# Three rounded passes for the query, key and value up-projections, and three weight splits moved ahead of their blocks

## What is computed

```python
# first layer: latent attention, sparse attention, gates, output projection
c_q = rmsnorm(c_q, mla_q_norm_g)                       # 512 x 384
q_a = einsum('bsr,re->bse', c_q, w_uq)                 # 8 heads x 96
c_kv = rmsnorm(c_kv, mla_kv_norm_g)                    # 512 x 256
k_nope = einsum('bsr,re->bse', c_kv, w_uk)             # 8 heads x 64
v_a = einsum('bsr,re->bse', c_kv, w_uv)                # 8 heads x 64
...
y = sigmoid(g_a) * (o_a @ w_o_a) + sigmoid(g_b) * (o_b @ w_o_b)
x = x + y @ w_out                                      # 1024 x 1024
...
# second layer: feed-forward with a 3-tap convolution
u = causal_dwconv(h @ ffn_up, ffn_dw)                  # 1024 -> 2 x 2816
y = (silu(u[..., 2816:]) * u[..., :2816]) @ ffn_down   # 2816 -> 1024
```

## Time and profile before

| | |
|---|---|
| median of 3 runs | 2231.27 us (2227.53 to 2238.28) |
| the profiled execution | 2231.33 us, span 2229.6 us |
| mean granted TensorE clock | 0.93 of full |
| PE busy | 1988.4 us, 89% of the span, 14734 matmuls |
| PE weight load (PEld) | 1689.8 us, 76% |
| DVE (VectorE) | 1311.2 us, 59% |
| ACT (ScalarE) | 945.0 us, 42% |
| POOL (GpSimd) | 711.1 us, 32% |
| HBM | 239.10 MB read, 116 GB/s over the span |

### The profile page before, as it was taken

How to read it: one execution, slowest core, us unless ns; L and a number is a source line. 1 busy time by engine, 2 the same in 40 slices (tenths; PEclk the granted TensorE clock), 3 DMA queues, 4 the chain that set the end, 5 groups by cost and what they waited for, 6 DMA issues and landing times. The chain is left out here.

```text
span 2229.6 us, 36859 instructions
## 1 busy us (share of the span) xinstructions
PE 1988.4 (89%) x14734; PEld 1689.8 (76%) x14734; DVE 1311.2 (59%) x1946; ACT 945.0 (42%) x1485; POOL 711.1 (32%) x378
## 2 busy tenths in 40 slices
PE   6999998799799997598999796688899989999797
PEld 4777644575677776598999575688689979999684
DVE  3779645432789897505999475565421167887402
ACT  4234258523788887522222543233333153232322
POOL 2433300131121111143433164421135425555441
PEclk9999988899899999699999897799789999999899
DMA  4222210022999998223223013210132212222231
GB/s 175 86 78 92 67 48 1 29 85 77 369 350 370 353 364 301 86 87 121 88 86 134 29 48 99 45 31 13 40 115 93 78 57 95 88 93 86 70 100 38
DMA packets 89378, 260.09 MB, mean 117 GB/s; under 512 B 26304, under 2 KB 27472, under 8 KB 88464
## 3 DMA queue, kind: packets, MB, share of 16 engines
q1 hardware_dynamic: 85488, 247.90, 32.1%
q0 software_dynamic: 3744, 10.11, 1.3%
HBM read 239.10 MB, written 18.87 MB: 116 GB/s over the span
## 5 line engine op out<-in xcount | busy, mean ns | idle before, releaser
L1546 DVE TENSOR_TENSOR moe_wlo<-moe_ring,moe_whi 128x1024 fp32r<-128x1024 f32 x198 | 234.0, 1219 | 43.4 <-ACT moe_whi L1542 40.5
L528 PE MATMUL acc<-h_xhi,h_whi 128*128 128x264 f32 x816 | 234.5, 287 | 13.1 <-DVE h_xlo L463 7.2
L528 PE MATMUL acc<-h_xlo,h_whi 128*128 128x264 f32 x816 | 233.5, 286 | 0.0
L528 PE MATMUL acc<-h_xhi,h_wlo 128*128 128x264 f32 x816 | 233.3, 286 | 0.0
L1542 ACT ACTIVATE moe_whi<-moe_ring 128x1024 fp32r<-128x1024 f32 x198 | 203.6, 1058 | 37.2 <-PE acc L1602 19.2
L528 PE MATMUL acc<-ff_xhi,ff_whi 128*128 128x258 f32 x704 | 200.8, 285 | 9.4 <-DVE ff_xlo L463 9.4
L528 PE MATMUL acc<-ff_xhi,ff_wlo 128*128 128x258 f32 x704 | 199.8, 284 | 0.0
L528 PE MATMUL acc<-ff_xlo,ff_whi 128*128 128x258 f32 x704 | 199.7, 284 | 0.0
L395 POOL TENSOR_TENSOR h_wlo<-ring,h_whi 128x1024 fp32r<-128x1024 f32 x49 | 117.5, 2400 | 201.7 <-ACT h_whi L387 201.7
L528 PEld LDWEIGHTS acc<-h_xhi,h_whi 128*128 128x128 f32 x816 | 156.1, 191 | 14.4 <-DVE h_xlo L463 8.3
L1986 DVE SCALAR_TENSOR_TENSOR acc<-cp,par,acc 128x528 f32<-128x528 f32 x232 | 159.2, 765 | 0.0
(11 more groups left out here) (506 smaller groups left out, 5158.4 us busy)
## 6 DMA issues: line engine op xcount, KB each, us to landing
ring<-slabs SPq DMA_DIRECT2D x213, 512.0 KB, 3.4
moe_ring<-moe_slabs SPq DMA_DIRECT2D x204, 512.0 KB, 5.7
tok_rows<-h_tok SPq DMA_DIRECT2D x5, 512.0 KB, 4.3
h_spill<-x2r SPq DMA_DIRECT2D x1, 2112.0 KB, 6.6
v_spill<-rw_v SPq DMA_DIRECT2D x1, 2112.0 KB, 7.4
y_spill<-cp SPq DMA_DIRECT2D x8, 264.0 KB, 4.6
rw_v<-v_spill SPq DMA_DIRECT2D x1, 2112.0 KB, 8.1
x2r<-h_spill SPq DMA_DIRECT2D x1, 2112.0 KB, 8.4
```

The costliest lines, as they stand in the source:

```text
L528: mm = nc.tensor.matmul(acc[j][0:rows, s, 0:t1 - t0], wp[:, at:at + rows], xp[:, t0:t1], start=(k == 0 and m == 0), stop=(k == kt - 1 and ...
L1546: tensor_tensor(wlo[u % AHEAD][:, :], ringm[u % RAW][:, :], whi[u % AHEAD][:, :].bitcast(F32), ALU.subtract).then_inc(w_lo[u % 2], 1)
```

## The change

1. The weights' buffers of the input block are made before `normalize("mix")`, and the first two c_q slabs are split there: ScalarE rounds the first after its eight squares and the second after the root; GpSimd subtracts both.
2. The up-projections take three rounded passes. The latents get an `Operand` each (`cq` 3 tiles, `ckv` 2). Slabs 1 and 2 of w_uq are split at the end of the gates' block, the other four (w_uq's third, two of w_uk, one of w_uv) inside the block, between read-outs on ScalarE and between the key copies on GpSimd.
3. w_out joins the block of w_o_a and w_o_b: `yo_xhi` and `yo_xlo` are made tile by tile as sums become ready, and TensorE goes on from w_o_b to w_out without a barrier.
4. ffn_down joins the block of ffn_up: 8 of the 22 `hid` tiles are split during ffn_up, 14 after its last tile; ffn_down's first two slabs are split before ffn_up's last tiles are read out.

Core of the diff (line numbers of the kernels differ by some lines after the first hunk):

```diff
-            if name not in ("w_uq", "w_uk", "w_uv", "wa_up", "g_up"):
+            if name not in ("wa_up", "g_up"):
...
+                        if split and enter:
+                            split[0].act(act, split[0].ahead(split[1])[0])
                         wait(act, sq_used, kt)
                         nc.scalar.activation(fold(std[:, :], t), A(1, t), ACT.Sqrt,
                                              bias=k0("eps", 1, eps)).then_inc(rooted, 1)
+                        if split and enter:
+                            split[0].act(act, split[0].ahead(split[1])[1])
...
                         tile_loop(act, w, [(name, KD, 8) for name in g_names], take)
+                        for n in w.ahead("w_uq"):
+                            w.act(act, n)
...
-                    pe_tiles(pe, None, "w_uq", 3, HEADS, lambda k: cc[:, k, :], T1, up_ready, up_out, rows=96)
-                    pe_tiles(pe, None, "w_uk", 2, HEADS, lambda k: cc[:, 3 + k, :], T1, up_ready, up_out, rows=64, first=8)
+                    pe_tiles(pe, w, "w_uq", 3, HEADS, cq, T1, up_ready, up_out, rows=96)
+                    pe_tiles(pe, w, "w_uk", 2, HEADS, ckv, T1, up_ready, up_out, rows=64, first=8)
...
+                            for m, (xp, wp) in enumerate(((ckv.hi, hi), (ckv.lo, hi), (ckv.hi, lo))):
...
+                    cq.act(act)
+                    ckv.act(act)
+                    tile_loop(act, w, [("w_uq", 3, 8), ("w_uk", 2, 8), ("w_uv", 2, 4)], take, ahead=3)
...
+                    cq.dve(dve)
+                    ckv.dve(dve)
                     for i in range(8):
                         dve.wait_ge(up_out, i + 1)
...
                     pe_tiles(pe, w, "w_o_b", 4, KD, bx, T1, oy_ready, oy_out, first=8)
+                    pe_tiles(pe, w, "w_out", KD, KD, yx, T1, xo_ready, xo_out, then=behind, prior=(oy_out, 16))
...
+                    for j, slab in enumerate(slab_range("w_o_b") + w.ahead("w_out")):
+                        w.act(act, slab)
+                        while n < min(2 * j - 3, KD):
+                            summed(n)
+                            n += 1
+                    for k in range(n, KD):
+                        summed(k)
...
                         if i >= 9:
                             both(i - 9)
+                        if i >= 12:
+                            yx.low(dve, i - 12)
                     both(7)
-                    dve.wait_ge(y_sum, 8)
+                    for k in range(4, KD):
+                        yx.low(dve, k)
...
                         pe_tiles(pe, w, "ffn_up", KD, 2 * NF, hx, T3, up_ready, up_read)
+                        pe_tiles(pe, wd, "ffn_down", NF, 8, dx, T1, dn_ready, dn_out, prior=(up_read, 2 * NF))
...
                             if i % 2 and i >= 3:
-                                silu(act, i // 2 - 1)
+                                silu(i // 2 - 1)
+                                if 0 <= i // 2 - 3 < EARLY:
+                                    round_hid(i // 2 - 3)
+                            if i >= 2 * NF - 3 and i < 2 * NF - 1:
+                                wd.act(act, down[i - 2 * NF + 3])
...
+                        for f in range(EARLY, NF):
+                            if f == NF - 4:
+                                silu(NF - 1)
+                                wd.act(act, down[2])
+                            round_hid(f)
...
+                            if i % 2 and 0 <= i // 2 - 4 < EARLY:
+                                dx.low(dve, i // 2 - 4)
+                        for f in range(EARLY, NF):
+                            dx.low(dve, f)
```

More of the change, by code:

```diff
@@ L588, in _ @@
                     def _(act):
-                        if split:
+                        if split and not enter:
                             for n in split[0].ahead(split[1]):
@@ L674, in first_block @@
                 with ExitStack() as mix:
+                    rstd_at = -(-nc.sbuf_base // 32) * 32
                     mix_rstd = sbt(mix, "mix_rstd", [P, T1])
+                    in_ctx = ExitStack()
+                    in_w = Weights(in_ctx, "in", side="right")
                     normalize("mix", lambda k: xt[:, k, :], lambda k: h[:, k, :], KD, T1, k0("mean1024"),
-                              None, left=mix_rstd, enter=(load, arrived))
+                              None, left=mix_rstd, enter=(load, arrived), split=(in_w, "c_q"))
                     with ExitStack() as att:
-                        w_out = attention_part(att, mix, xt, h, k1, mix_rstd, c1_here)
-                    out_projection(xt, h, w_out)
+                        attention_part(att, mix, xt, h, k1, mix_rstd, c1_here, in_ctx, in_w, c1_at, rstd_at)
                 x1 = first.enter_context(nc.sbuf_tensor("x1_tok", [P, 4, D], F32, side="right"))
@@ L1022, in _ @@
                         w.all_pool(pool, g_names)
+                        for n in w.ahead("w_uq"):
+                            w.pool(pool, n)
                     @b.sync
@@ L1069, in _, with rests @@
                 def _(pool):
+                    slabs_of_ups = slab_range("w_uq", "w_uk", "w_uv")
+                    def rests(first, end):
+                        for n in slabs_of_ups[first:end]:
+                            w.pool(pool, n)
+                        pool.wait_ge(lo_made, split_rank[n] + 1)
+                    rests(2, 4)
                     for hd in range(HEADS):
                         link("pool", pool, nc.gpsimd.tensor_copy(ka[64:96, hd, :], kr[64:96, :]))
+                        if hd == 2:
+                            rests(4, 5)
+                        if hd == 5:
+                            rests(5, 6)
                 @b.sync
@@ L1101, in _ @@
                     w.begin(act, ["w_o_a"], ax, bx)
-                    w.all_act(act, ["w_o_a", "w_o_b"])
-                    for n in w.ahead("w_out"):
-                        w.act(act, n)
+                    w.all_act(act, ["w_o_a"])
+                    n = 0
+                    for j, slab in enumerate(slab_range("w_o_b") + w.ahead("w_out")):
[3 more added lines that the diff above has]
+                            n += 1
@@ L1186, in _ @@
                 def _(pool):
-                    w.all_pool(pool, ["w_out"])
+                    w.all_pool(pool, ["w_o_a", "w_o_b", "w_out"])
                 @b.sync
@@ L3254, in _ @@
                                 w.pool(pool, n)
-                            if f == NF - 1:
-                                wd.pool(pool, wd.ahead("ffn_down")[0])
+                            if f >= NF - 2:
+                                wd.pool(pool, down[f - NF + 2])
                             pool.wait_ge(silued, f + 1)
```

198 lines of the change are left out of this document (95 added, 103 removed).

## The result

| | us | against before, same calls |
|---|---|---|
| changed kernel, first comparison, median of 7 | 2213.26 (2208.58 to 2215.68) | ratio 0.9928, 95% interval 0.9900 to 0.9956 |
| changed kernel, second comparison, median of 12 | 2217.48 (2211.56 to 2220.92) | ratio 0.9948, 0.9932 to 0.9963 |
| kernel before, the same two | 2231.27 and 2230.6 | |
| profiled execution after | 2211.80, span 2210.0, clock 0.941 | before: 2231.33, 2229.6, 0.930 |

The kernel is faster, by 13 to 18 us, where 18.3 was forecast. The total hides more than it shows. I put both traces side by side at read-outs that exist in both, and give each stage the change of its length; w_out's and ffn_down's tiles are counted from the first read-out to the eighth. A second trace of the changed kernel stands beside the first.

What follows compares the result with a forecast made beforehand. TensorE, busy for 89% of the span, was taken as the bound, gained on by fewer passes and closed holes. Terms -4.2 - 0.9 - 3.6 - 9.6 = -18.3 us from 2231.33 gave 2213 us, range 2205 to 2221.

Steps and rivals of the forecast that it cites:

- Term 1, start: Kernel start to first input tile: first read-out near 31.8 us instead of 36.03, -4.2 us; ends -5.0 and -2.5.
- The cover: Start: rounding the first slab and ScalarE's table load end at 15.2, ahead of the root, covered by TensorE's sums; cost nothing.
- both collisions: Start: VectorE's `in_xlo` and `h`, held by GpSimd's slab subtractions at 2.60 and 2.85 us; `in_xlo` then takes 0.68 us.
- Term 2, up-projections: Up-projections: 144 short matmuls save 8.9 us, a later start and low clock cost most of it; -0.9 us, ends -5 and +2.
- The start of TensorE: Up-projections: TensorE starts at 270.0 instead of 263.74, behind the first two w_uq slabs' rounding and subtraction; +6.3 us.
- the low clock: Up-projections: the slow 1.2 GHz restart behind the hole at the block's head, charged at 1.7 us.
- my plus end: Up-projections: VectorE's rotations, held by slab subtractions, near the block's end at 303.5, TensorE done at 304.5; +2 us.
- Term 3, w_out: w_o_b to w_out: hole and low clock go, 6.5 at most, 2.9 given back; -3.6 us, ends -6.5 and -1.2.
- the one collision that was charged: w_out: its second slab's subtraction falls among the last five low parts and TensorE waits once; 2.9 us given back.
- Term 4, ffn_down: ffn_up to ffn_down: first tile out at 2085.3 instead of 2094.91, -9.6 us; ends -14 and -6.
- Rival D: ffn_up: eight early low parts hit GpSimd's subtractions and VectorE becomes the bound; +12.2 us there, 2235 us in all; chance 0.03.
- a change of a stage in between: Stages between, attention or the experts: a change of more than a microsecond would mean something unseen acts.

Runs made afterwards that it cites:

- The early split: Changed kernel with the first two w_uq slabs rounded and subtracted behind the gates' tiles 13 and 14, not the last: 2210.61 us, ratio 0.9908.
- the pads of 480 and 992: Changed kernel with w_uq's first two slabs split earlier and 480 or 992 bytes ahead of the right-side weight tiles: 2203.04 and 2199.64 us.

## Why the prediction was right, and where only its sum was

The forecast of 2213 us met the first median by 0.3 us and the second by 4.5. The sum is partly luck, and says so term by term.

- **Term 1, start:** -3.5 and -3.2 for -4.2, but -4.2 when it is counted from the root (16.26 us for 20.45). The cover held, and both collisions are gone; the rest is when TensorE's sums ahead of the root are done, which differs between executions of either kernel.
- **Term 2, up-projections:** +1.7 for -0.9. The passes save about 8.2 us (144 steps of 0.232 instead of 0.227), not 10.4: that would take three quarters of a plain product, 0.217 us a pass, and a rounded pass is longer than such a quarter. The start of TensorE, forecast at +6.3, was +3.8. I had VectorE's first low part held until both subtractions were done, and it was held behind the first one only. The steps that failed are the ones behind it: I let TensorE run without a further wait, and it waits 1.5 us for the second collision and 1.2 us for two later slabs; the low clock costs 3.1 us (13 steps at 0.43 us, 2.5, and 0.6 in the first ones) where I charged 1.7 (the row behind attention's hole gives 1.8 to 2.0, 4.00 us for 9 matmuls of 0.227 or their 3.86 busy ones). That makes +1.4 of the +1.7. The early split shows that the place was right: this head is where the gain went. VectorE as the end of the block, my plus end, comes to within 0.13 us of ScalarE's last read-out once the head is gone, but no run here has it as the end.
- **Term 3, w_out:** -3.8 for -3.6, with the one collision that was charged.
- **Term 4, ffn_down:** -8.0 and -9.5 for -9.6; in seven further kernels with this code 19.4 or 19.5 us, where the forecast said 19.4. That hit is partly luck as well. I had the tile hang on VectorE's last low part, ready 18.7 us behind ffn_up's last read-out, and 0.7 us for the rest. The last part is ready at 17.6 us, because the parts follow one another every 0.60 us, and the tile is out 1.9 us behind it, because TensorE, after 3.55 us of waits for earlier parts, still has matmuls to do. The two errors cancel: with the early parts it is TensorE that sets the first read-out. The 21.1 us of the first trace hold 3.4 us of low clock, which I had not charged. Rival D, VectorE as the bound of ffn_up, is excluded: 5.76 us a tile, unchanged. (Its +12.2 should read +12.0, eight times 1.5; nothing hangs on it.)
- **What I had costed at nothing and was not:** the place of the weight tiles, +5.5. I read the diff's `side="right"` as a matter of room, a term put at nothing without a reason. The figures were in the trace of before: w_o's matmuls, with weights on the right, follow one another every 0.233 us there, the input projections' every 0.227.
- **What filled the gap:** the recurrence, -11.9 in the first trace, by its own clock. The prediction said that a change of a stage in between would show something I had not seen; it showed two such things of opposite sign.

The stages that the change can reach sum to -8.2 us in the first trace and -9.4 in the second (start, input tiles, up-projections, both w_out rows, ffn and its tiles). The medians give -13 to -18. Some 4 us or more of the gain are in no stage that I can tie to the change. The executions of before spread from 2216 to 2238 us and those of the changed kernel from 2209 to 2221; a clock that is on average a little better in attention and the recurrence would make up the difference. For it, the mean granted clock has a median of 0.933 in the executions of the kernel before and of 0.941 and 0.939 in the two series of the changed one. 0.006 of 2230 us is 27 us less at the half clock, and all stages but attention, the experts and the recurrence account for 7 and 13 us of that in the two traces. Against it, the traces do not place it there: attention averages 126.3 us over the four traces with the old code and 126.7 over the ten with the new, the recurrence 363.5 and 364.5. Where the rest was won stays open.

## What to carry to other kernels

A sum that comes out right proves nothing about its terms: put the two traces side by side at read-outs that both have, and look first at the stages in which nothing was changed. A tile that is moved in SBUF is a change to every instruction that reads it, so compare the spacing of its matmuls, not only their number. When a plain product is replaced by cheaper passes, the work that prepares its operands needs a place of its own beside earlier TensorE work; here that place, two read-outs earlier, was worth 6 us and the passes without it nothing.

## What the runs showed of the hardware

- A rounded matmul of 512 columns at the 2.4 GHz level starts every 0.227 us if its weight tile and its operand tile begin at the same place within 512 bytes, and every 0.229, 0.232 or 0.233 us if the weight tile begins 64, 128 or 32 bytes short of it (tiles of 24 matmuls: 5.44; 5.49, 5.57, 5.60). Moving both by 128 bytes leaves 5.44, moving one makes 5.58. The Trainium skill's "SBUF — State Buffer", section "SBUF: two separate sides", says that on the engines' side only the port pair of VectorE and GpSimd causes contention and TensorE waits on no one; here the time of TensorE's matmuls depends by up to 3% on where its own two tiles lie. That its two reads hinder each other would explain it; no run shows it. No distance of 256 bytes was run, and the rule is shown for 512 columns alone. w_out's tiles, whose two operand halves lie differently, took 5.63 us before, 5.55 or 5.65 in kernels with the changed placement (5.65 in three that leave w_out's code as it is) and 5.50 with the pads of 480 and 992; I have no rule for them.
- The same page's word for the loser of the port pair, "fully blocks", fits VectorE's addition in w_out (2.86 us for 0.68, beside 2.92 of GpSimd). The other way round it was longer: a GpSimd subtraction of 2.4 us took 7.17 us beside a row of VectorE subtractions of 0.68.
- The same hole of 4.8 us in the same code (last gate tiles to w_uq) was followed by 6 to 14 matmuls at the 1.2 GHz spacing in five traces, 1.2 to 2.7 us lost; the two traces of one and the same kernel have 13 and 14.
